# Splitting the recurrence gates' block products into three products of rounded parts

## What is computed

```python
xc = depthwise_conv(cx, conv_w)                  # width 4, causal
xf = xc + conv_b
xb = xf.reshape(B, S, C_BLOCKS, C_BLOCK_DIM)     # 8 blocks of 128
r  = sigmoid(einsum('bshi,hij->bshj', xb, wa) + ba)
ig = sigmoid(einsum('bshi,hij->bshj', xb, wx) + bx)
log_a = -RG_C * r * softplus(-lam)
a = exp(log_a)
u = sqrt(-expm1(2.0 * log_a)) * ig * xf
h = associative_scan(combine, (a, u))            # h_t = a_t h_(t-1) + u_t
```

## Time and profile before

| | |
|---|---|
| median of 3 runs | 586.78 us |
| lowest, highest | 586.18, 586.83 us |
| span of the profiled execution | 584.0 us |
| PE busy | 575.8 us, 99% of the span |
| DVE busy | 416.3 us, 71% |
| ACT busy | 384.3 us, 66% |
| POOL busy | 73.8 us, 13% |

### The profile page before, as it was taken

The page is one execution under the profiler, slowest core; times in us unless marked ns, Lnnn a source line. Parts: engine busy times, 40 slices in busy tenths (PEclk is TensorE's granted clock), DMA queues, the critical chain, the costliest instruction groups (busy, mean ns, idle before and its releaser), DMA issues.

```text
span 584.0 us, 9717 instructions
## 1 busy us (share of the span) xinstructions
PE 575.8 (99%) x3868; PEld 532.9 (91%) x3868; DVE 416.3 (71%) x647; ACT 384.3 (66%) x581; POOL 73.8 (13%) x77
## 2 busy tenths in 40 slices
PE   8999999999999999999999999999999999999995
PEld 7999989999999898889988999999899998888985
DVE  6879589447977684567557874799997974766663
ACT  6863685278397575657666847969758837566764
POOL 4130005001003900100000001112120200100002
PEclk9999999999999999999999999999999999999999
DMA  9856354446715963564445545326544463356201
GB/s 290 255 181 227 108 181 145 145 145 216 218 72 162 289 200 144 177 229 172 145 145 176 184 162 181 128 109 224 208 145 145 167 233 133 118 217 220 105 2 72
DMA packets 51856, 98.88 MB, mean 169 GB/s; under 512 B 1732, under 2 KB 7140, under 8 KB 51812
## 3 DMA queue, kind: packets, MB, share of 16 engines
q1 hardware_dynamic: 50628, 96.95, 49.2%
q0 software_dynamic: 1024, 1.05, 0.7%
q10 hardware_dynamic: 160, 0.27, 0.1%
HBM read 96.16 MB, written 1.05 MB: 166 GB/s over the span
## 4 chain that ended last, share of the span: by engine, by line
PE 97%; DMA 1%; DVE 1%; ACT 0%; issue 0%; SPq 0%; DVEq 0%; ACTq 0%
PE proj L1775 17%; PE proj L1776 17%; PE proj L1777 17%; PE proj L1794 11%; PE proj L1795 11%; PE proj L1796 11%; PE head L2010 4%; PE head L2086 1%; PE head L2193 1%; PE head L1854 1%; DMA x_residual<-in_x_dram 1%; PE head L1987 1%; PE head L2055 1%; PE head L2224 1%; PE head L2095 1%; PE proj L1816 0%
## 5 line engine op out<-in xcount | busy, mean ns | idle before, releaser
L1090 DVE TENSOR_TENSOR w_lo<-raw_weights,w_hi 128x1024 fp32r<-128x1024 f32 x174 | 224.3, 1304 | 105.9 <-ACT w_hi L515 104.2
L515 ACT ACTIVATE w_hi<-raw_weights 128x1024 fp32r<-128x1024 f32 x174 | 182.1, 1056 | 118.1 <-PE proj L1777 60.5
L1775 PE MATMUL proj<-xT_hi,w_hi 128*128 128x256 f32 x752 | 215.9, 287 | 0.0
L1777 PE MATMUL proj<-xT_hi,w_lo 128*128 128x256 f32 x752 | 212.8, 283 | 0.0
L1776 PE MATMUL proj<-xT_lo,w_hi 128*128 128x256 f32 x752 | 212.7, 283 | 0.0
L1775 PEld LDWEIGHTS proj<-xT_hi,w_hi 128*128 128x128 f32 x752 | 144.2, 192 | 0.6
L1776 PEld LDWEIGHTS proj<-xT_lo,w_hi 128*128 128x128 f32 x752 | 144.2, 192 | 0.5
L1777 PEld LDWEIGHTS proj<-xT_hi,w_lo 128*128 128x128 f32 x752 | 144.2, 192 | 0.0
L1794 PE MATMUL proj<-w_hi,y_hi 128*128 128x512 f32 x176 | 69.4, 394 | 0.0
L1796 PE MATMUL proj<-w_lo,y_hi 128*128 128x512 f32 x176 | 68.5, 389 | 0.0
L1795 PE MATMUL proj<-w_hi,y_lo 128*128 128x512 f32 x176 | 68.5, 389 | 0.0
(11 more groups left out here) (297 smaller groups left out, 775.6 us busy)
## 6 DMA issues: line engine op xcount, KB each, us to landing
raw_weights<-in_ev_w_in_dram SPq DMA_DIRECT2D x15, 2048.0 KB, 8.6
raw_weights<-in_od_w_in_dram SPq DMA_DIRECT2D x12, 2048.0 KB, 7.9
raw_weights<-in_ev_w_out_dram SPq DMA_DIRECT2D x4, 2048.0 KB, 7.7
raw_weights<-in_xa_wkv_dram SPq DMA_DIRECT2D x4, 2048.0 KB, 7.6
raw_weights<-in_od_w_out_dram SPq DMA_DIRECT2D x4, 2048.0 KB, 7.8
raw_weights<-in_xa_wq_dram SPq DMA_DIRECT2D x2, 2048.0 KB, 9.2
raw_weights<-in_xa_wo_dram SPq DMA_DIRECT2D x2, 2048.0 KB, 8.3
x_residual<-in_x_dram SPq DMA_DIRECT2D x2, 512.0 KB, 3.8
```

Source lines behind the costliest of these rows:

```text
L515: act.activation(ring_quarter(w_hi, n, q), raw_quarter(n, q), ACT.Copy).then_inc(hi_ready, 1)
L1090: dve.tensor_tensor(ring_quarter(w_lo, n, q), raw_quarter(n, q), ring_quarter(w_hi, n, q).bitcast(F32), ALU.subtract).then_inc(lo_ready, 1)
L1775: pe.matmul(dst, wh[:, k, :], x_hi[:, k, :], start=(k == 0), stop=False)
L1777: last = pe.matmul(dst, wl[:, k, :], x_hi[:, k, :], start=False, stop=(k == KC - 1))
```

## The change

The block products are made as the projections are: three products of rounded parts in place of one unsplit f32 product.

- POOL gets `gate_weights_split(g)` for both groups, right behind `y_low(3)`: it waits for the weights and for the last quarter of "XA0 o", copies 128x1024 weights to fp32r (`rg_hi`, which are blocks 8 to 15 of `y_hi`), drains, and subtracts (`rg_lo`, blocks 8 to 15 of `y_lo`).
- ACT gets `xf_high(u)` twice in each group: 128x512 of the convolution's output to fp32r, in blocks 0 to 7 of `y_hi`.
- POOL gets `xf_low(g, u)` twice in each group: 128x512 elements, the output less its high part.
- PE makes 24 products for 8 in each group, and waits for `rg_split` and `xf_split` in place of the DMA and of `xf_ready`.

The names `rg_split`, `xf_hi_ready` and `xf_split` are new semaphores.

```diff
+        rg_hi, rg_lo = (y[:, 8:16, :].rearrange("p k t -> p (k t)").rearrange("p (m h c) -> p m h c", m=4, h=4)
+                        for y in (y_hi, y_lo))
...
+            def gate_weights_split(g):
+
+                pool.wait_ge(rg_landed[g], 32)
+                pool.wait_ge(quarter_used, 4 * slab("XA0", "o") + 4)
+                pool.tensor_copy(rg_hi[:, 2 * g:2 * g + 2], rg_w[:, 2 * g:2 * g + 2])
+                pool.drain()
+                pool.tensor_tensor(rg_lo[:, 2 * g:2 * g + 2], rg_w[:, 2 * g:2 * g + 2],
+                                   rg_hi[:, 2 * g:2 * g + 2].bitcast(F32), ALU.subtract).then_inc(rg_split, 1)
+
+            def xf_low(g, u):
+
+                pool.wait_ge(xf_hi_ready, 2 * g + u + 1)
+                c = 4 * g + 2 * u
+                pool.tensor_tensor(y_lo[:, c:c + 2, :], conv_out(g)[:, 2 * u:2 * u + 2, :],
+                                   y_hi[:, c:c + 2, :].bitcast(F32), ALU.subtract).then_inc(xf_split, 1)
...
             y_low(3)
+            gate_weights_split(0)
+            gate_weights_split(1)
+            xf_low(0, 0)
+            xf_low(0, 1)
             gated_input(0)
             decay_square(0)
+            xf_low(1, 0)
+            xf_low(1, 1)
             gated_input(1)
...
+                def xf_high(u):
+
+                    act.wait_ge(xf_ready, 2 * g + u + 1)
+                    c = 4 * g + 2 * u
+                    act.activation(y_hi[:, c:c + 2, :], conv_out(g)[:, 2 * u:2 * u + 2, :], ACT.Copy
+                                   ).then_inc(xf_hi_ready, 1)
...
                 ahead(z, 1)
+                xf_high(0)
                 ahead(z, 2)
+                xf_high(1)
...
             def gates(g):
-                pe.wait_ge(rg_landed[g], 32)
+                pe.wait_ge(rg_split, g + 1)
...
-                            pe.wait_ge(xf_ready, 2 * g + h // 2 + 1)
-                        last = pe.matmul(head[2 * m + h // 2][:, S * (h % 2):S * (h % 2) + S], rg_w[:, 2 * g + m, h, :],
-                                         conv_out(g)[:, h, :], start=True, stop=True)
+                            pe.wait_ge(xf_split, 2 * g + h // 2 + 1)
+                        dst = head[2 * m + h // 2][:, S * (h % 2):S * (h % 2) + S]
+                        wh, wl = rg_hi[:, 2 * g + m, h, :], rg_lo[:, 2 * g + m, h, :]
+                        pe.matmul(dst, wh, y_hi[:, 4 * g + h, :], start=True, stop=False)
+                        pe.matmul(dst, wh, y_lo[:, 4 * g + h, :], start=False, stop=False)
+                        last = pe.matmul(dst, wl, y_hi[:, 4 * g + h, :], start=False, stop=True)
```

More of the change, by code:

```diff
@@ L232, in hybrid_trunk @@
         xf_ready = sem("xf_ready")
+        rg_split = sem("rg_split")
+        xf_hi_ready = sem("xf_hi_ready")
+        xf_split = sem("xf_split")
         gates_psum = sem("gates_psum")
```

## The result

| | before | after |
|---|---|---|
| median | 586.81 us | 593.37 us |
| lowest, highest | 586.18, 588.97 us | 593.17, 594.79 us |
| profiled execution: time, span | 586.83, 584.0 us | 594.79, 592.7 us |
| mean granted clock in it | 0.999 | 0.993 |

The runs of before are the three of the table ahead and a fourth (588.97 us). The ratio is 1.0115, with an interval of 1.0094 to 1.0135: the change costs 6.6 us where 4.4 were forecast. The profiled execution of after is the longest of its four by 1.2 us, and its clock is the lowest (the three others have 0.995).

What follows compares the result with a forecast made beforehand. PE was taken to bound the kernel, without slack. Span 584.0 + 3.1 (wait before turn_rows) + 1.3 (gates, gains included) = 588.4 us; with 2.8 between median and span, 591.2 us, range 587.8 to 595.5.

Steps and rivals of the forecast that it cites:

- the first wait: Before turn_rows: POOL's weights' split takes turns with DVE's norm, leaving PE idle 3.1 us (bounds 0.7 to 4.6).
- the term for both gates: End of gates(1): +1.3 us against before, PE's gain in both groups included; bounds -0.5 to +4.1.
- the rival: After PE idles before turn_rows, its clock halves, adding 1.6 to 3.1 us: 592.8 to 594.3 us; chance 0.14.
- What bounds the kernel: PE, busy 575.8 of 584.0 us, has no slack: spared products shorten and waits lengthen the kernel by their length.
- The gain: In gates, 24 split products starting 0.12 us apart replace 8 unsplit: 0.58 us spared per group, 1.16 in all.
- the second wait: Inside gates(1): PE waits 2.45 us for POOL's low part, behind a convolution made 1.25 us later.
- The rule that I set aside: At the norm: DVE tensor_scalar and POOL exclude each other whatever the size, holding line 1098 too; 0.8 us more.
- Nothing here speaks for or against it: On the clock falling while PE waits: the trace shows no long PE idleness and no lower grant; chance 0.14.
- The chain on ACT and DVE behind group 0 isn't any sooner: Between gates(0) and gates(1): it runs on from the first sigmoids, whose input is ready when it was before.
- The quarter is needed by PE some 8 us later and the root waits for DVE anyway: nothing.: ACT's new copies stand before a weights' quarter and a root; claimed to cost nothing.

Runs made afterwards that it cites:

- The products alone: Kernel before with 24 split-style products per group on ready but wrong operands, no engine splitting anything: 585.71 us, ratio 0.9989.
- the run with the wait covered: Changed kernel plus 28 unread products of 128x256 on PE directly before turn_rows: 592.12 us, ratio 1.0088.

## Why the prediction was right, point by point

The direction, the two waits and their places were right, and the time lies in the range. The forecast was 2.2 us below the median. Of that 0.6 is the first wait, 1.4 the clock (by medians) and 0.5 a late quarter behind the gates; the term for both gates was 0.4 too dear, which makes 2.1. The time lies in the band of the rival and not in that of the forecast (592.8 to 594.3, not 588.9 to 592.7), and partly by luck: the clock alone, at 1.4 us, would have given 592.6.

- **What bounds the kernel.** Right: nothing that PE met was swallowed. The idle times, the clock and the shifts add up to the difference of the spans within 0.1 us.
- **The gain.** Right to the digit: 24 products of gates(0) start 0.12 us apart and end 0.58 us sooner against their start. The products alone gave 0.9 of 1.16 us, since a quarter was then late, so what PE is spared doesn't shorten the kernel by its whole length everywhere.
- **The first wait, 3.1 us forecast, 3.7 measured.** The mechanism (POOL's split of the weights beside the norm, in turns) was right, and the weights alone bring it. The term was made of wrong pieces. The casts took 1.97 and 1.04 us, of which 1.1 us of the first were spent behind DVE's subtraction (until 322.11): about 0.9 and 1.0 of their own, where I took 1.3 each. The first subtraction came 2.8 us late, because of a drain that I had priced at nothing. (I knew the pause from decay_square and had it as a bound on the second wait, so at the wrong place.) In the other direction, with POOL late, DVE's third subtraction wasn't pushed (line 1126 took 1.23 us at 323.53). And line 1134 was held, 0.91 us in place of its 0.17.
- **The rule that I set aside.** I worked out that line 1098 (1134 now) would run beside POOL, since a row of 128x1 had. It was held, and its neighbour 1132 (128x2, two inputs) too, for 2.08 us. The Trainium skill, page "SBUF — State Buffer", section "Who interferes with whom", says that such an instruction and GpSimd exclude each other for its whole length, and names no size from which on they do; this case's trace agrees for the tensor_scalar and the tensor_tensor of 128x2. The tensor_scalar of 128x1 remains an exception that no run here explains. The size is not what decides in any case, since the reciprocal of 128x2 wasn't held with the early drain. The 0.8 us that the rule would have added would have come closer, though in other pieces than these.
- **The clock.** This is the rival with a chance of 0.14, priced at 1.6 to 3.1 us on top, and it came true: 2.7 us in the profiled execution, about 1.4 in the medians, which is below that price. The step that failed is the weight that I gave it. "Nothing here speaks for or against it" was true of the trace, whose longest idle time behind 10 us was 0.1 us, but it was no reason for a low chance. The Trainium skill, page "TensorE: Matmul & The Clock Gate", Part 1, says that an idle TensorE falls to half its clock; the trace agrees (0.51 behind 3.55 us of idleness), and the run with the wait covered (1.00) shows the cause. It does not follow every time: one of the four runs with only the weights' split kept 0.999.
- **The second wait.** Its chain was right in every link. The term of +1.3 us was +0.9, and PE waited 1.5 us (from 390.66, when the seventh product was due, to 392.15) and not 2.45. Half of that difference is no gain: PE came 0.5 us later to the gates, by the wait for the quarter at 384.12, and would have stood there until 392.15 in any case. The other half is the chain's. The step that failed is "The chain on ACT and DVE behind group 0 isn't any sooner": ACT's copies of C x in group 1 wait for PE (line 964 at 378.16, 6.67 us later than line 937 before, where PE is 6.65 later), and what follows on ACT had the 0.58 us of group 0's gain with it. That is why the first low part came 0.56 us sooner, not in the midst of the convolution's second half but at its head. It held line 1608 there for 1.0 us. Together with the new place of decay_square (0.1) and DVE 0.3 us sooner the second half started 0.86 us late (387.05 against 378.96 + 7.23), where 1.25 were forecast. (That the instructions of line 1613 too are held where POOL falls among them is seen in group 0, where six took 3.67 in place of 2.79 us without harm.) The second low part, which I had held for 0.55 us by DVE's subtraction and then taking 1.25, was done 1.59 us after the high part where 1.8 were forecast.
- **"The quarter is needed by PE some 8 us later and the root waits for DVE anyway: nothing."** Wrong. The ring of weights was late twice in the changed kernel, 0.5 us each, and in every experiment that makes the new parts, by up to 1.2 us of idle time at once. The quarters behind ACT's copies were not the ones that came late. The root does wait for DVE, but DVE's `one_minus_a2` was held 1.07 us by the second low part, which the sum left out, and the root and the subtractions behind it moved with it past the ring's 0.44 us of slack.

## What to carry to other kernels

Where one engine is 99% busy, moving work to an idle one isn't free: look at what else has to run in that engine's port and at that moment, since here 14 us of new work on a 13% busy POOL brought 5 us of idle time and cost 1.4 us more by the clock that fell behind the longest of them. A gain of 0.2% on the busy engine needs slack in all of the engines that feed it: here the ring behind the gates had 0.44 us, and whatever drew DVE and PE further apart than that came out as waits. Count a wait by the starts behind it and not by its idle time, which showed 0.3 us where 0.5 were lost. And when an instruction is late with nothing in the profile to hold it, move the synchronisation ahead of it to where there is time: one early drain won back 3 us here, nearly half of the loss.

## What the runs showed of the hardware

- **The first drain behind POOL's own DMAs costs 2.8 us.** It came ahead of decay_square before (2.8 us late), ahead of the weights' subtraction after (2.79 us), stayed there when 32 empty instructions were put ahead (2.79 us), and was gone from both kernels when a drain stood right behind the DMAs. A drain ahead of them cost 0.15 us. No run leaves the DMAs out, and what the drain waits for stays open.
- **Half a clock behind 3.5 us of idleness, in most executions and not all.** It lasted for 6.8 us (332.0 to 338.9), the first 1.2 of them still idle, and made transposes take 3.33 us in place of 1.67. With 1.9 us of idleness the profiled execution kept 1.00.
- **POOL holds short instructions of DVE too, but not all**: a tensor_tensor of 128x2 took 2.08 us beside it and a tensor_scalar 0.91 us; a reciprocal of 128x2 took its usual 0.17 us and a tensor_scalar of 128x1 0.15 us.
- **The ring of weights has 0.44 us of slack behind gates(1)**, 0.43 to 0.45 us in the ten traces in which it was used up.
- Left open: why two executions of one kernel behind the same wait have a full and a half clock, and how often the clock falls behind 2 us of idleness: one of four runs with the early drain has a lower mean clock.
